# All v rows of gather passes 2, 4 and 6 to TensorE, in buffers of 4 picks of 32 tokens

## The chip, the cores and the metric

One core of one Trainium2 chip runs one program that is launched once. The time is device microseconds of that core, the median of the runs that were made; the trace is of one profiled execution of the same program. Engines are called PE (TensorE), PEld (its weight loads), DVE (VectorE), ACT (ScalarE), POOL (GpSimd) and SP (SyncE); the 16 DMA engines of the core are taken together.

## The reference, cut to what matters

A small model of 256 tokens, width 1024, all in float32: an mLSTM block, two PEER feed-forward layers, a latent attention block, gates, and a tail with a sparse attention, a convolution, a linear attention and a dense feed-forward. The change is in the PEER layers, which pick 128 single-neuron experts for each token (8 heads by 16 best) out of 16384:

```python
def peer_ffn(x, w_q, sub_keys, u, v):
    ...                     # scores of product keys, top 16 of each head: expert_idx, gates
    def expert_block(args):                       # a block of 128 tokens
        xb, eb, gb = args
        ub = jnp.take(u, eb, axis=0)              # 128 tokens x 128 picks x 1024
        act = jax.nn.gelu(jnp.einsum('thkd,td->thk', ub, xb), approximate=False)
        vb = jnp.take(v, eb, axis=0)              # the same number of rows of v
        return jnp.einsum('thk,thkd->td', gb * act, vb)
```

## The kernel before

The 256 tokens are two tiles of 128. With two layers, two tiles and the tables u and v there are eight **gather passes** of 128 gathers each, in the order (layer 0, tile 0, u), (0, 0, v), (0, 1, u), (0, 1, v), (1, 0, u), (1, 0, v), (1, 1, u), (1, 1, v). The code numbers them n = 0 to 7; the texts say pass 1 to pass 8, so that passes 2, 4, 6 are n = 1, 3, 5. One gather (`issue`, line 946) is one indirect DMA that POOL issues: partition p gets the row of 4 KB of the pick c of token p, so a buffer holds one pick of 128 tokens, 0.524 MB. There are `SLOTS` = 12 buffers, used in turn over all 1024 gathers; POOL waits, before gather i, until gather i - 12 has been used: on `row_used` if DVE used it, on `pe_used` if PE did. SP loads the dense weights in an order of their own into a ring of three buffers, beside the gathers.

A u row is one DVE instruction (`use_row`, line 991): the product with the token's x, which ACT has put into the PSUM tensor XP, summed to one number. A v row on DVE (lines 993 and 995) is XP = XP + row * gate. In passes 2, 4 and 6 (`SHARED`) half of the rows, four of every eight, are PE's: ACT writes a 128x128 diagonal matrix of the gates of this pick (`act_share`, line 1031, four of them in turn), and PE multiplies it with the row into two banks, accA and accB, by two matmuls of 512 columns (`pe_share`, line 1016 on; every float32 matmul is recorded as two MATMULs with a LDWEIGHTS each, so a buffer is four). Pass 8 is DVE's alone. `dve_sums` closes a pass: Y = ALPHA * X + XP, plus the two banks.

Around the passes the order is written out by hand in phases at whose ends PE, ACT and DVE meet. `weigh` lies in the last part of a u pass and turns the 128 sums of a token into gates in two halves of 64. `peer_route` projects the queries (four blocks of 32 matmul calls), scores them and picks the experts of the layer above (`picks`), with the v rows of passes 4 and 6 beside it: PE takes six rows, a block of queries, a block of scores, six rows, and so on. `peer_done` adds and normalises, and beside pass 2 it holds the scores and picks of the second tile. While DVE does its own steps, it takes a row now and then (`gather_some`), so that rows and steps alternate on it.

## Time and profile before

| | |
|---|---|
| median of 3 runs | 2252.76 us (2241.89 to 2260.28) |
| span of the profiled execution | 2259.6 us |
| instructions in it | 17114 |
| busy: PE, PEld, DVE, ACT, POOL | 1527.2, 879.4, 1450.5, 323.1, 985.0 us |
| DMA | 760.62 MB, of which gathers 536.94 MB |
| passes 1 to 8 begin at (first gather issued) | 208.45, 406.87, 595.72, 805.20, 1013.29, 1228.22, 1436.24, 1683.64 us |
| last gather issued | 1914.87 us |

The profiled execution has its span, 2259.6 us, as its time; it is 6.8 us (0.3%) above the median and 0.7 us below the longest of the three runs. Times inside the trace are counted from the start of the span.

### The profile page before, as it was taken

Reading aid. Unit: us, or ns where it says so; the run is one execution under the profiler, and the core shown is the slowest. Engines: PE = TensorE matmul, PEld = TensorE weight load, DVE = VectorE, ACT = ScalarE, POOL = GpSimd, SP = SyncE. Lnnn points to the kernel's source line nnn. Section 1 sums busy time; section 2 is a strip of 40 time slices with the busy share of each in tenths; the row PEclk is TensorE's granted clock in tenths of the full one; section 3 lists DMA queues with packets and bytes.
Section 4 is the critical chain, followed back from the end, with each engine's and each line's share of the span. In section 5 each row is a group of like instructions: output and inputs, shape, how many; then the busy total and the mean of one; then the engine's idle time right before and its main releaser. Section 6 shows DMA issues by size and latency. Waiting matters only on the chain. (4 is left out here: it accounts for less than half of the span.)

```text
span 2259.6 us, 17114 instructions
## 1 busy us (share of the span) xinstructions
PE 1527.2 (68%) x5282; PEld 879.4 (39%) x5282; DVE 1450.5 (64%) x3168; ACT 323.1 (14%) x778; POOL 985.0 (44%) x1058
## 2 busy tenths in 40 slices
PE   8987600467656539776573897666576656899998
PEld 7446600222225225422341552235252232376453
DVE  1236898779587875678688468786978676444101
ACT  1220100011112111111120111111321000123111
POOL 0102466667665555566455456653446444000000
PEclk9989855688867669987766899778767877899999
DMA  7436999999999999999999999999989999973672
GB/s 260 85 117 245 394 408 409 337 360 370 371 379 403 404 406 358 361 365 367 407 399 405 365 342 368 375 401 386 391 293 403 399 398 399 366 243 130 242 260 93
DMA packets 268005, 760.62 MB, mean 337 GB/s; under 512 B 21295, under 2 KB 46590, under 8 KB 267275
## 3 DMA queue, kind: packets, MB, share of 16 engines
q0 software_dynamic: 147456, 536.94, 61.8%
q1 hardware_dynamic: 120458, 222.60, 27.8%
q8 instruction: 43, 0.70, 0.1%
q14 instruction: 48, 0.39, 0.0%
HBM read 756.84 MB, written 2.62 MB: 336 GB/s over the span
## 5 line engine op out<-in xcount | busy, mean ns | idle before, releaser
L946 POOL DMA_INDIRECT ROWS<-in_peer_u,IDX x512 | 483.3, 944 | 455.5 <-DVE ROWS L991 266.9
L946 POOL DMA_INDIRECT ROWS<-in_peer_v,IDX x512 | 487.8, 953 | 357.2 <-PE bank L292 121.4
L991 DVE SCALAR_TENSOR_TENSOR ROWS<-ROWS,XP 128x1024 f32<-128x1024 f32 x512 | 602.3, 1215 | 23.7 <-issue 12.3
L995 DVE SCALAR_TENSOR_TENSOR XP<-ROWS,GATE,XP 128x1024 f32<-128x1024 f32 x316 | 405.8, 1284 | 155.9 <-DMA ROWS<-in_peer_v,IDX 133.7
L292 PE MATMUL bank<-ROWS,DG 128*128 128x512 f32 x774 | 380.0, 649 | 94.2 <-DMA ROWS<-in_peer_v,IDX 78.5
L292 PE MATMUL bank<-ring,XT 128*128 128x512 f32 (+6 forms) x912 | 392.7, 589 | 62.3 <-DMA ring<-in_ffn_w_up 32.0
L292 PEld LDWEIGHTS bank<-ring,XT 128*128 128x128 f32 x912 | 185.6, 214 | 249.9 <-issue 179.4
L292 PEld LDWEIGHTS bank<-ROWS,DG 128*128 128x128 f32 x774 | 157.5, 209 | 309.8 <-issue 201.8
L292 PE MATMUL bank<-XT,ring 128*128 128x128 f32 (+2 forms) x1504 | 209.4, 301 | 57.1 <-issue 27.4
L292 PEld LDWEIGHTS bank<-XT,ring 128*128 128x128 f32 (+1 forms) x1504 | 198.3, 204 | 71.8 <-issue 35.7
L307 PE MATMUL bank<-CN,X 128*128 128x128 f32 x128 | 27.1, 384 | 184.9 <-issue 90.7
L391 POOL TENSOR_TENSOR stat<-stat,CN 128x1 f32<-128x1 f32 x5 | 2.8, 552 | 304.6 <-DVE stat L1870 132.5
L292 PE MATMUL bank<-KEYT,QP 128*128 128x128 f32 x128 | 22.0, 333 | 162.9 <-DVEq L472 159.5
L1031 ACT ACTIVATE DG<-CN,GATE 128x128 f32<-128x128 f32 x192 | 71.0, 397 | 326.0 <-PE bank L292 198.6
L307 PEld LDWEIGHTS bank<-CN,X 128*128 128x128 f32 x128 | 22.5, 202 | 197.8 <-issue 197.8
L292 PE MATMUL bank<-ring,FT 128*128 128x512 f32 x132 | 67.2, 669 | 27.6 <-DMA ring<-in_ffn_w_down 19.9
L292 PEld LDWEIGHTS bank<-KEYT,QP 128*128 128x128 f32 x128 | 20.6, 246 | 164.9 <-issue 160.7
L1171 DVE MAX8 TV<-bank 128x8 f32<-128x128 f32 x64 | 14.3, 284 | 87.8 <-PE bank L292 86.7
L292 PE MATMUL bank<-VEC,CN 13*128 13x512 f32 x76 | 46.3, 756 | 30.6 <-DVEq L472 23.3
L292 PE MATMUL bank<-ROWS,XT 128*128 128x512 f32 (+3 forms) x176 | 65.3, 528 | 1.4 <-ACT XT L1847 1.4
L292 PEld LDWEIGHTS bank<-ring,FT 128*128 128x128 f32 x132 | 28.0, 217 | 65.6 <-issue 52.3
L886 POOL TENSOR_SCALAR_AFFINE_SELECT ROWS<-ROWS 128x128 f32<-128x128 f32 x16 | 4.3, 294 | 112.9 <-ACT ROWS L778 112.9
(408 smaller groups left out, 1461.6 us busy)
## 6 DMA issues: line engine op xcount, KB each, us to landing
ring<-in_peer_w_q SPq DMA_DIRECT2D x16, 2048.0 KB
ring<-in_ple_w_gate SPq DMA_DIRECT2D x9, 2048.0 KB
ring<-in_ffn_w_gate SPq DMA_DIRECT2D x8, 2048.0 KB
ring<-in_ffn_w_up SPq DMA_DIRECT2D x7, 2048.0 KB
ring<-in_a_w_in SPq DMA_DIRECT2D x6, 2048.0 KB
ring<-in_w_in SPq DMA_DIRECT2D x6, 2048.0 KB
ring<-in_ffn_w_down SPq DMA_DIRECT2D x6, 2048.0 KB
ROWS<-in_peer_u,IDX POOLq DMA_INDIRECT x512
```

The source lines that it names most:

```text
L292: return mm(out_, lhsT, rhs, start=start, stop=stop, skip_group_check=True)
L307: last = tr(b[:, j * P:(j + 1) * P], src[:, tt, (g + j) * P:(g + j + 1) * P], ident)
L391: G.tensor_tensor(cells, cells, CN[:, at:at + cells.shape[1]], ALU.pow).then_inc(*tick(name_out))
L886: ins = G.affine_select(block_, block_, [[1, P]], ALU.is_ge, zero, base=0, channel_multiplier=-1)
L946: G.indirect_dma_start(ROWBUF[slot(n, c)][:, :], None, tables[table], bass.IndirectOffsetOnAxis(IDX[:, tt, c:c + 1], axis=0)).then_inc(row ...
L991: V.scalar_tensor_tensor(row, row, 1.0, XP[:, :], ALU.mult, ALU.mult, accum_out=ACTV[:, tt, c:c + 1]).then_inc(row_used, 1)
L995: V.scalar_tensor_tensor(XP[:, :], row, gate, XP[:, :], ALU.mult, ALU.add).then_inc(row_used, 1)
L1031: A.activation(DG[tensor_used(n, x) % DIAGS][:, :], ident, ACT.Copy, scale=GATE[:, tt, c:c + 1]).then_inc(diag_ready, 1)
L1171: V.max(vals[:, k, at:at + 8], source(k)).then_inc(*tick("dve_step"))
```

## The change

Passes 2, 4 and 6 get another layout of a buffer and no longer use DVE or ACT for their rows.

- A gather of these passes takes, for partition 32k + t, the pick 4g + k of token 32q + t: four picks (k) of 32 tokens (q fixed), so that four buffers q = 0 to 3 hold four picks of all 128 tokens. The index table for it, `IDXV`, is made ahead of the pass: DVE writes the picks as floats once more (`IDXF`), PE moves them with 16 small matmul calls by 32 columns of the identity (`pe_to_quads`), and DVE copies them to integers. POOL waits for that (`picks_turned`) before the pass.
- The gates are moved in the same way in two halves, and DVE spreads them with four instructions of 128x1024 elements a pass (`dve_spread`): for each buffer a 128x32 matrix that has the gate of partition 32k + t in column t.
- PE multiplies such a 128x32 matrix with the buffer into the 32 partitions 32q to 32q + 31 of accA and accB. `pe_share` now goes by groups of four buffers: it waits until all four have landed, makes four calls into the four partition groups of accA, then four into those of accB, each of which raises `pe_used`.
- DVE takes no row of these passes, ACT makes no diagonals, and `dve_sums` adds ALPHA * X straight to the banks. ACT writes the x of the next u pass into XP as soon as the last u pass is used, and DVE takes two u rows before it adds.
- PE takes the first two groups in `weigh`, then four groups between two blocks of queries, and in `peer_done` of pass 2 it takes the rest after the scores.
- A part of the constants that only the first phase uses is loaded into the gather buffers instead of its own memory.

```diff
-        SHARED = (1, 3, 5)
+        BY_PE = (1, 3, 5)
         def by_pe(n, c):
-            return n in SHARED and c % (2 * RUN) >= RUN
+            return n in BY_PE
...
+                picks = IDXV if n in BY_PE else IDX
                 G.indirect_dma_start(ROWBUF[slot(n, c)][:, :], None, tables[table],
-                                     bass.IndirectOffsetOnAxis(IDX[:, tt, c:c + 1], axis=0)).then_inc(row_in[slot(n, c)], 16)
+                                     bass.IndirectOffsetOnAxis(picks[:, tt, c:c + 1], axis=0)).then_inc(row_in[slot(n, c)], 16)
...
+        def pe_to_quads(src, name):
+            m = src.shape[1] // GROUP
+            b = job(name)
...
+            for k in range(GROUP):
+                for q in range(GROUP):
+                    last = mul(b[QUAD * k:QUAD * k + QUAD, q:GROUP * m:GROUP], ident[:, QUAD * q:QUAD * q + QUAD],
+                               src[:, k:GROUP * m:GROUP], True, True)
...
+        def dve_spread(n, half):
...
+            for x in (2 * half, 2 * half + 1):
+                gates = result(name)[:, QUAD * (x % 2):QUAD * (x % 2) + QUAD]
+                V.tensor_tensor(spread(tt, x), con("spread").unsqueeze(1).broadcast_to([P, QUAD, QUAD]),
+                                gates.unsqueeze(2).broadcast_to([P, QUAD, QUAD]), ALU.mult).then_inc(spread_ready, 1)
...
+        def pe_share(n, g0=0, g1=PICKS // GROUP):
+            accs, tt = (result("accA"), result("accB")), passes[n][1]
+            for g in range(g0, g1):
...
+                PE.wait_ge(spread_ready, 4 * (n // 2) + x + 1)
+                weights = spread(tt, x)
+                for q in range(GROUP):
+                    PE.wait_ge(*arrived(n, GROUP * g + q))
+                for q in range(GROUP):
+                    to, row = slice(QUAD * q, QUAD * q + QUAD), ROWBUF[slot(n, GROUP * g + q)]
+                    last = mul(accs[0][to, :], weights[:, j + q, :], row[:, 0:512], first, end)
...
+                        mul(accs[1][to, :], weights[:, j + q, :], row[:, 512:1024], first, end).then_inc(pe_used, 1)
-                A.activation(DG[tensor_used(n, x) % DIAGS][:, :], ident, ACT.Copy, scale=GATE[:, tt, c:c + 1]).then_inc(diag_ready, 1)
...
         def dve_sums(n):
+            V.wait_ge(*nth("x_copied", 2))
+            gather_begin(n + 1)
+            gather_some(2)
             V.wait_ge(pe_used, tensor_used(n))
             for i, name in enumerate(("accA", "accB")):
                 V.wait_ge(bank_ready(name), turn(name))
-                y = Y[:, tt, i * 512:(i + 1) * 512]
-                V.tensor_tensor(y, y, result(name)[:, :], ALU.add).then_inc(bank_free(name), 1)
+                s = slice(i * 512, (i + 1) * 512)
+                V.scalar_tensor_tensor(Y[:, tt, s], X[:, tt, s], ALPHA, result(name)[:, :], ALU.mult, ALU.add).then_inc(bank_free(name), 1)
...
         def weigh(block, st, n):
+            if to_pe:
+                @block.tensor
+                def _(pe):
+                    for i, half in enumerate(halves):
+                        pe.wait_ge(*nth("gate_done", i + 1))
+                        pe_to_quads(GATE[:, tt, half], f"gv{i}")
+                    pe_share_begin(n + 1)
+                    pe_share(n + 1, 0, 2)
...
         def peer_route(block, st, l, tiles, tag, KEYT, KEYT1):
                 for e in range(5):
-                    if l == 1:
-                        pe_share(beside, 6 * e, 6 * e + 6)
+                    if l == 1 and e > 0:
+                        pe_share(beside, 4 * e - 2, 4 * e + 2)
...
                 if l == 1:
-                    pe_share(beside, 30)
+                    pe_share(beside, 18)
```

## Rows read from the trace of the kernel before

**Rows 1.** Page: busy engines; DMA share in tenths and GB/s, 40 slices
```profile
PE 1527.2 (68%) x5282; PEld 879.4 (39%) x5282; DVE 1450.5 (64%) x3168; ACT 323.1 (14%) x778; POOL 985.0 (44%) x1058
...
DMA  7436999999999999999999999999989999973672
GB/s 260 85 117 245 394 408 409 337 360 370 371 379 403 404 406 358 361 365 367 407 399 405 365 342 368 375 401 386 391 293 403 399 398 399 366 243 130 242 260 93
```

**Rows 2.** Windows, one for each pass 1, 2, 3, 4, 6, 8
```profile
core 0: us, PE busy (x) PEld busy (x) DVE busy (x) ACT busy (x) POOL busy (x), PEclk, DMA share, GB/s
208.45:406.87 198.42, 47.60 (x379) 45.60 (x378) 173.87 (x376) 9.98 (x17) 121.87 (x128) 0.63 1.03 400
406.87:595.72 188.85, 125.92 (x272) 54.40 (x272) 136.14 (x315) 24.63 (x65) 123.06 (x129) 0.85 0.95 356
595.72:805.20 209.48, 110.37 (x350) 65.63 (x350) 168.23 (x345) 30.74 (x66) 120.03 (x128) 0.69 1.02 395
805.20:1013.29 208.09, 154.03 (x536) 86.23 (x536) 134.54 (x316) 26.55 (x71) 122.11 (x129) 0.88 0.98 370
...
1228.22:1436.24 208.02, 157.38 (x536) 87.38 (x536) 135.29 (x317) 26.77 (x71) 122.65 (x129) 0.87 0.96 362
...
1683.64:1937.90 254.26, 156.45 (x322) 70.75 (x320) 182.43 (x168) 15.37 (x29) 119.95 (x128) 0.79 1.03 400
```

**Rows 3.** Windows: in pass 1, in pass 2, and the two parts of pass 4
```profile
320.00:360.00 40.00, 0.00 (x0) 0.00 (x0) 37.50 (x64) 0.26 (x1) 26.70 (x29) 0.50 1.03 409
...
430.00:440.00 10.00, 10.00 (x41) 5.93 (x40) 7.20 (x24) 1.55 (x4) 2.92 (x4) 0.98 0.64 220
...
805.00:945.00 140.00, 106.52 (x443) 67.46 (x444) 78.95 (x189) 16.87 (x45) 76.89 (x82) 0.86 0.98 376
945.00:1013.29 68.29, 47.52 (x95) 18.77 (x93) 55.79 (x127) 9.68 (x26) 45.22 (x47) 0.91 0.97 358
```

**Rows 4.** Page, costliest groups: busy us, mean ns of one, idle before
```profile
L946 POOL DMA_INDIRECT ROWS<-in_peer_v,IDX x512 | 487.8, 953 | 357.2 <-PE bank L292 121.4
L991 DVE SCALAR_TENSOR_TENSOR ROWS<-ROWS,XP 128x1024 f32<-128x1024 f32 x512 | 602.3, 1215 | 23.7 <-issue 12.3
L995 DVE SCALAR_TENSOR_TENSOR XP<-ROWS,GATE,XP 128x1024 f32<-128x1024 f32 x316 | 405.8, 1284 | 155.9 <-DMA ROWS<-in_peer_v,IDX 133.7
L292 PE MATMUL bank<-ROWS,DG 128*128 128x512 f32 x774 | 380.0, 649 | 94.2 <-DMA ROWS<-in_peer_v,IDX 78.5
```

**Rows 5.** Waits of POOL, pass 2, then pass 4: us, times, longest
```profile
POOL ROWS L946 <- PE bank L292: 21.3, 12, 5.3
...
POOL ROWS L946 <- PE bank L292: 48.7, 19, 8.9
```

**Rows 6.** Timeline of PE, then of POOL, in pass 2
```profile
485.44 4.88 PE L292 MATMUL bank<-ROWS,DG 128*128 128x512 f32 x11
492.53 7.13 PE L292 MATMUL bank<-ROWS,DG 128*128 128x512 f32 x16 [2.21 <-issue]
...
492.02 0.94 POOL L946 DMA_INDIRECT ROWS<-in_peer_v,IDX  x1 [0.30 <-issue]
497.06 0.94 POOL L946 DMA_INDIRECT ROWS<-in_peer_v,IDX  x1 [4.10 <-PE bank L292]
```

**Rows 7.** Timeline of PE and PEld, linear attention, first and second tile
```profile
1619.03 0.65 PE L292 MATMUL bank<-STB,QG 128*64 128x256 f32 x2
...
2041.77 0.65 PE L292 MATMUL bank<-STB,QG 128*64 128x256 f32 x4
...
2041.77 0.20 PEld L292 LDWEIGHTS bank<-STB,QG 128*64 128x64 f32 x4
```

**Rows 8.** Instructions nearest to the new ones: group by form, and timeline
```profile
L1224 DVE TENSOR_TENSOR QP<-HALFF,CN 128x1024 f32<-128x1024 f32 x16 | 19.5, 1218 | 0.8 <-remote 0.7
...
2040.74 1.10 PE L292 MATMUL bank<-GVS,AM 128*128 128x64 f32 x8
```

**Rows 9.** Timeline of PE in pass 4: a block of queries
```profile
838.19 6.53 PE L292 MATMUL bank<-XT,ring 128*128 128x128 f32 x57
```

More of the change, by code:

```diff
@@ L46 @@
 VECTORS = 13
-DIAGS = 4
+GROUP = 4
+QUAD = P // GROUP
 NH, NKV, HD = 8, 2, 64
@@ L122, in con @@
             at, n = cwhere[name]
+            if at >= early_at:
+                return CN_EARLY[0:rows_, at - early_at:at - early_at + n]
             return CN[0:rows_, at:at + n]
@@ L489, in end_phase @@
             base.update(count)
-            jobs.clear()
+            for name in [k for k in jobs if not (held and k in ("accA", "accB"))]:
+                del jobs[name]
         PE = nc.tensor
@@ L901, in build @@
         ACTV = sb("ACTV", [P, TT, PICKS], F32, peer_mem)
-        DG = [sb(f"DG{i}", [P, P], F32, peer_mem) for i in range(DIAGS)]
+        IDXF = sb("IDXF", [P, PICKS], F32, peer_mem)
+        IDXV = sb("IDXV", [P, TT, PICKS], I32, peer_mem)
         ROWBUF = [ROWS[:, s, :] for s in range(SLOTS)]
@@ new lines, in pe_turn_picks, with dve_turn_picks, spread @@
+        def pe_turn_picks(l, tt):
+            PE.wait_ge(S("pick_numbers"), 2 * (TT * l + tt) + 2)
+            pe_to_quads(IDXF[:, :], "turned")
+        def dve_turn_picks(l, tt):
+            V.wait_ge(bank_ready("turned"), turn("turned"))
+            V.tensor_copy(IDXV[:, tt, :], result("turned")[:, 0:PICKS]).then_inc(bank_free("turned"), 1)
+            V.wait_ge(bank_free("turned"), turn("turned"))
+            V.sem_inc(S("picks_turned"), 1)
+        def spread(tt, x):
+            part = Y[:, tt, :] if x == 2 else later["spread"][:, min(x, 2), :]
+            return part.rearrange("p (j t) -> p j t", t=QUAD)
@@ L1233, in best_pairs @@
                 step_done()
+                V.tensor_scalar(IDXF[:, ks], EX[:, 0, :], float(l * NEXP), None, ALU.add).then_inc(S("pick_numbers"), 1)
                 V.tensor_scalar(IDX[:, tt, ks], EX[:, 0, :], float(l * NEXP), None, ALU.add).then_inc(picks_ready, 1)
@@ L2813, in peers @@
                     phase(mla, tt, KNT, VM, KRT)
-                    phase(weigh, 2 + 2 * tt)
-                    phase(peer_route, 1, (tt,), f"1{tt}", KEYT1, None)
-                    phase(peer_done, 3 + 2 * tt)
+                    with ExitStack() as st:
+                        later["spread"] = sb("SPREAD", [P, 3, D], F32, st)
+                        phase(weigh, 2 + 2 * tt)
+                        phase(peer_route, 1, (tt,), f"1{tt}", KEYT1, None)
+                        phase(peer_done, 3 + 2 * tt)
             keys1_mem.close()
```

102 lines of the change are left out of this document (55 added, 47 removed).

## The prediction

> **What bounds the kernel now.** I read the page's slices first, then windows by pass, then who waits for whom. No engine is busy for more than 68% of the span, but the DMA line stands at 8 or 9 tenths in every slice from the fifth to the thirty-fourth [rows 1]: from the first gather at 208.45 us to the end of pass 8 the kernel is paced by transfers. The windows tell how well. Passes 1, 3 and 8, whose rows are DVE's alone, move 395 to 400 GB/s at a share of 1.02 or 1.03; passes 2, 4 and 6, which share their rows between DVE and PE, move 356, 370 and 362 GB/s at 0.95 to 0.98 [rows 2]. The best stretch moves 409 [rows 3], which is 0.524 / 409 = 1.28 us a gather. So the time that this change can win is the difference of these rates in three passes, and the work that it takes off DVE is not itself on the path.
>
> The ceiling of it: a pass's bytes are its window by its rate, 67.2, 77.0 and 75.3 MB. At 403 GB/s (between 400 and 409) they take 167, 191 and 187 us, where they take 188.9, 208.1 and 208.0 now [rows 2]. That is 22 + 17 + 21 = **60 us**, and no version with the same bytes wins more in these passes.
>
> Why the transfers fall short: POOL waits for PE to give back buffers, 21 us in pass 2 and 49 us in pass 4 [rows 5]. PE takes 380.0 / 192 = 1.98 us for a buffer [rows 4], 7.13 us for a run of four at the full clock [rows 6], and between runs it has a block of queries, 6.5 us for the bulk of one [rows 9]; at the start of pass 2 such a wait leaves the DMA engines at 0.64 and 220 GB/s for 10 us [rows 3]. A second cause is POOL itself. An issue takes 0.94 us and 0.30 us lie before the next [rows 6], so POOL gives at most one gather in 1.24 us, against 1.28 us of transfer: once the queue has run low it hardly fills again. And some of its pauses are not about buffers. The one before 497.06 us is put down to PE, but counting issues against uses, the buffer needed is that of gather 47, a PE row, and PE was through with it at 485.44 + 4.88 = 490.3 us, 6.7 us earlier [rows 6]. By the same count over the whole trace, pauses without a missing buffer cost 21 us in pass 2, 10 in pass 4 and 17 in pass 6; buffers cost 9, 39 and 33. I don't know what makes the former.
>
> **The change, part by part.**
>
> DVE loses 3 x 64 = 192 rows of 1.284 us [rows 4], 247 us. In passes 2, 4, 6 DVE is busy for 135 of 189 to 208 us [rows 2] and falls to some 55 plus the new steps. This is no gain by itself: what was late there was the buffer.
>
> PE had 64 buffers a pass, about 127 us at 1.98. It now has 128 buffers in 32 groups of 16 MATMULs of the same 512 columns. If the four partition groups ran one after the other, a group would cost the 7.13 us of [rows 6]. The trace has one place where matmuls write two partition groups of a bank side by side: the linear attention makes one call of 64 output rows for the first tile, and for the second tile two calls into partitions 0 to 63 and 64 to 127. The first takes 0.65 us for 2 MATMULs, the second 0.65 us for 4 [rows 7]. Two groups cost what one costs, in float32, in one bank. For four groups there is no row; the bounds are 7.13 / 4 = 1.8 us if all overlap and 7.13 / 2 = 3.6 us if only two do. I take 1.8 to 2.4, near full overlap; what matters is that both ends are below the 4 x 1.28 = 5.1 us in which four buffers land. So PE needs 58 to 115 us a pass for rows, less than now, and stops being late. At a granted clock of 0.50 (1.2 GHz) the ends double to 3.6 and 7.1 us; the latter alone would be too slow, but PE without pauses has clocks of 0.86 to 0.98 here [rows 3].
>
> A rule of the Trainium skill speaks against it. TensorE: Matmul & The Clock Gate, Part 3, says that weight loads overlap matmuls in flight only when the row group differs, and here all four groups use all rows. The loads of the two-group case run under its matmuls, 0.20 us of loads inside 0.65 us [rows 7], so this trace does not agree. By the rule sixteen loads at 0.20 / 4 = 0.05 to 0.1 us would add 0.8 to 1.6 us to a group, as an estimate, and the sum would stay, since 4 us is still below 5.1. The same part gives 2.38 times the throughput for three column groups; that would be about 3 us for a group, again with the sum unchanged.
>
> Between two blocks of queries PE now has 16 buffers, 7 to 10 us, and queries and scores of about 9, so 16 to 19 us, while 16 buffers and 2 MB of weights take 16 x 1.28 + 5 = 25.5 us to land. The longest absence of PE, some 10 us, is covered by the eight buffers that are then under way or to be filled (8 x 1.28 = 10.2 us, plus the weights). So the 39 and 33 us of buffer waits go, in as far as the DMA engines can use it.
>
> New on DVE: four spreads a pass, 12 x 1.22 us by the nearest row, the one-hot products of the picks [rows 8], 15 us in all. Two of them lie before the last 60 u rows of passes 1, 3, 5, with a wait for PE's 32 small matmuls of at most 0.14 us [rows 8], up to 4.4 us less the two rows taken meanwhile. DVE gets some 4 us late and wins 0.14 us a row back (a u row recurs after 1.14 us when nothing is missing); 12 buffers cover what is left. Bounds: 0 and 3 x 4 = 12 us. I take 2. Were DVE as late as in the middle of pass 7, all 12 would count.
>
> At the turn from u to v, PE starts only after the second half of the gates, and only when four rows have landed. The last u row of pass 1 is used at about 423 us, gate and move take about 4 us, the first group about 3.6 at the low clock: buffers come back at about 431 us, four at once, while the transfers under way last until about 437. Bounds 0 and 5 us a pass, I take 1. In return the 5 us wait near 430 us of pass 2 falls away [rows 3].
>
> ACT loses 192 diagonals, which nobody misses. The second write of the picks, the float copy and the turned indices lie on DVE and PE ahead of passes that start 100 us later or more; in front of pass 1 they add 0.3 us. POOL waits for `picks_turned`, with everything behind it on its queue, but by then this is long raised. POOL issues the same 1024 gathers of the same bytes, and SP one more transfer of the constants, under the first phase.
>
> **The sum.** What decides is how much of the 60 us POOL lets through. Where weights share the engines (until about 945 us in pass 4, 140 us at 376 GB/s [rows 3]) few gathers are needed and the DMA bound is reached: 140 x (1 - 376/403) = 9 us, and in pass 6, at 362 over the whole pass [rows 2], 14. In the stretches of gathers alone, all of pass 2 and the last 68 us of passes 4 and 6, POOL's own pauses stay: pass 2 becomes 128 x 1.24 + 21 = 180 us and wins 9; the two ends run at 358 now, and take 0 to 8 us less each, I take 4. That is 9 + 9 + 14 + 8 = 40. The earlier start of u rows at the end of passes 2, 4, 6 (DVE takes two before it waits for PE) gives perhaps 1 each, and the spreads and the turns cost 2 + 3: **38 us**. The profiled span of 2259.6 becomes 2221.6; against the median of 2252.8 it is **2215 us**.
>
> **The rivals.**
>
> *The full ceiling.* The pauses that have no missing buffer may come from the alternation with PE: pass 3 has few of them. Then 60 less 5 gives 2198 us. For it: pass 1 runs at 409 for 40 us with POOL undisturbed. Against: pass 1 has such pauses too, and its rate sinks towards its end.
>
> *POOL is the bound anyway.* If POOL's pauses grow where it no longer waits for buffers, to what pass 2 shows today (356 GB/s), passes 4 and 6 hardly move, and the spreads and turns cost their 12 and 15 us bounds in part: 10 us less, 2243 us, within 1%.
>
> *The partition groups don't overlap.* Two groups of 64 do; four of 32 might not. Then a group costs 7.13 us and a pass 32 x 7.13 = 228 us, plus 5 in pass 2, and plus PE's other 27 us and the drains, 32, in passes 4 and 6: 233 + 260 + 260 = 753 against 605 us now, 148 us more, **2401 us**. It decides as soon as a group with its share of queries takes over 6.4 us, which is 5.1 us and a quarter of the weights. This is also the case in which the change does not do what it says.
>
> **How the numbers follow.** The middle case 0.57 (2200 to 2228), the full ceiling 0.11, POOL bound 0.21 (2231 to 2262), no overlap 0.08 (2330 to 2420), and 0.03 for something slower by 20 to 60 us at the turns. A measurement here can tell 1%, 22 us, from nothing. Below 2230: 0.70. Within 1%: 0.19. Above 2275: 0.11. The range leaves out no overlap and a little on either side: 2190 to 2258.
>
> **What would show it.** In the profile after: L995 with 128 rows instead of 320; MATMULs of 128*32 with four starting nearly together and a group in about 2 us; POOL's waits for PE in pass 4 falling from 49 us to under 10; windows of passes 2, 4, 6 of about 180, 195 and 190 us at 375 to 400 GB/s; passes 1, 3, 5, 7, 8 as long as before. The prediction is wrong if a group takes over 5 us, if POOL's issues come more than 1.45 us apart without waits, or if the last u rows of passes 3 and 5 are used so late that the DMA share falls at the turn.

## The result, and the profile after

The changed kernel takes 2269.12 us (median of 7 runs, 2261.97 to 2278.42), the kernel before 2259.91 us in 7 runs beside it. The ratio is 1.007, with an interval of 1.0049 to 1.0091: slower by 0.7%. 2215 us was forecast, 54 us less than measured, and 2269 lies above the range. The profiled execution took 2261.97 us (span 2260.2), the shortest of the seven.

The page after, busy engines and GB/s in 40 slices, against [rows 1]:

```profile
PE 1431.8 (63%) x6338; PEld 796.0 (35%) x6338; DVE 1233.9 (55%) x2996; ACT 253.1 (11%) x586; POOL 983.4 (44%) x1058
...
GB/s 259 83 131 240 395 408 390 341 363 372 376 376 404 405 370 376 353 365 349 405 403 397 371 329 372 367 399 399 391 307 403 401 398 401 382 252 120 245 257 105
```

DVE lost 217 us of work and PE 95, and the rates (GB/s) are those of before. The windows of passes 1 to 8, in the columns of [rows 2]:

```profile
207.19:409.86 202.67, 51.92 (x443) 49.38 (x442) 173.11 (x380) 10.06 (x17) 122.23 (x129) 0.64 1.02 392
409.86:596.47 186.61, 94.78 (x556) 24.57 (x560) 64.58 (x255) 1.38 (x3) 121.42 (x128) 0.73 0.97 361
596.47:812.56 216.09, 116.24 (x426) 69.60 (x416) 168.41 (x346) 29.62 (x64) 120.29 (x129) 0.66 1.02 395
812.56:1019.07 206.51, 118.95 (x824) 58.17 (x824) 66.95 (x261) 4.85 (x9) 121.44 (x128) 0.78 0.96 363
1019.07:1236.27 217.20, 125.35 (x446) 73.82 (x438) 169.57 (x346) 31.32 (x64) 120.27 (x129) 0.67 1.00 390
1236.27:1442.45 206.18, 123.07 (x808) 58.88 (x808) 66.67 (x261) 4.85 (x9) 122.07 (x128) 0.75 0.95 359
1442.45:1681.49 239.04, 144.80 (x652) 99.81 (x652) 192.51 (x472) 48.99 (x143) 121.60 (x129) 0.69 1.01 380
1681.49:1917.40 235.91, 151.14 (x305) 69.11 (x306) 168.89 (x158) 15.37 (x29) 119.20 (x127) 0.78 1.02 393
```

Passes 2, 4 and 6 were to fall to 180, 195 and 190 us at 375 to 400 GB/s. They take 186.6, 206.5 and 206.2 us at 361, 363 and 359, some 2 us less each than [rows 2]. Passes 1, 3 and 5 are 4.3, 6.6 and 2.3 us longer, pass 7 8.4 us shorter, and the last gather is issued at 1917.40 us instead of 1914.87.

The work itself is as the change says. Costliest groups of the page, against [rows 4]:

```profile
L955 POOL DMA_INDIRECT ROWS<-in_peer_v,IDXV x384 | 364.9, 950 | 240.2 <-issue 97.0
...
L298 PE MATMUL bank<-ROWS,SPREAD 128*32 128x512 f32 (+1 forms) x1158 | 192.0, 784 | 151.0 <-DMA ROWS<-in_peer_v,IDXV 131.7
...
L1006 DVE SCALAR_TENSOR_TENSOR XP<-ROWS,GATE,XP 128x1024 f32<-128x1024 f32 x127 | 163.7, 1289 | 65.8 <-DMA ROWS<-in_peer_v,IDX 63.8
...
L298 PE MATMUL bank<-ROWS,Y 128*32 128x512 f32 x384 | 70.5, 856 | 64.6 <-DMA ROWS<-in_peer_v,IDXV 57.6
```

The two PE lines are one kind of work: a quarter of the weights lies in the memory of Y. Together they are PE's 96 groups of 16 MATMULs.

Waits of POOL in pass 2, then pass 4, against [rows 5]:

```profile
POOL ROWS L955 <- remote: 19.4, 11, 3.2
POOL ROWS L955 <- PE bank L298: 11.8, 10, 4.2
...
POOL ROWS L955 <- PE bank L298: 43.8, 13, 10.7
```

The 48.7 us of waits in pass 4 were to fall under 10 and are 43.8, in fewer and longer pieces (13 up to 10.7 us, where there were 19 up to 8.9). POOL's pauses are of two kinds, and two stretches show them. First PE, in pass 4, timeline:

```profile
843.01 5.36 PE L298 MATMUL bank<-ROWS,SPREAD 128*32 128x512 f32 x48
858.28 3.64 PE L298 MATMUL bank<-ROWS,SPREAD 128*32 128x512 f32 x16 [9.91 <-DMA ROWS<-in_peer_v,IDXV]
861.85 7.82 PE L298 MATMUL bank<-XT,ring 128*128 128x128 f32 x64
869.51 1.06 PE L298 MATMUL bank<-KEYT,QP 128*128 128x128 f32 x8
870.50 5.36 PE L298 MATMUL bank<-ROWS,SPREAD 128*32 128x512 f32 x48
```

PE does three groups in 5.36 us, since they have long landed, and then waits 9.91 us for the fourth, whose gathers POOL could issue only from 845.19 us on, with buffers of the first of the three. With the fourth done at 861.9 PE goes away for queries and scores until 870.5, and gives nothing back before 872.4. POOL fills the four buffers of that fourth group (862.15 to 865.88) and stands still until 872.67. So such a block finds four free buffers, not eight. POOL's gaps at these places, from issue to issue, are 6.6, 6.8, 9.9 and 11.7 us in pass 4 and 6.6, 8.2, 11.2 and 11.8 us in pass 6, against 1.245 us without a wait.

Second, POOL, DVE and PE in pass 2, where no queries are:

```profile
496.14 0.94 POOL L955 DMA_INDIRECT ROWS<-in_peer_v,IDXV  x1 [0.30 <-issue]
499.94 0.94 POOL L955 DMA_INDIRECT ROWS<-in_peer_v,IDXV  x1 [2.85 <-remote]
...
494.04 0.27 DVE L1241 FIND_INDEX8 BI<-BV,SC 128x8 uint32<-128x112 f32 x1
499.57 0.23 DVE L1266 TENSOR_TENSOR GATE<-BV 128x64 f32<-128x64 f32 x1 [5.26 <-remote]
...
492.56 1.92 PE L298 MATMUL bank<-ROWS,SPREAD 128*32 128x512 f32 x16 [1.97 <-DMA ROWS<-in_peer_v,IDXV]
497.67 3.52 PE L298 MATMUL bank<-ROWS,SPREAD 128*32 128x512 f32 x16 [3.18 <-DMA ROWS<-in_peer_v,IDXV]
```

The gather at 499.94 needs the first buffer of the group that starts at 492.56 and by its MATMUL records ends at 494.48. This is a pause "without a missing buffer", as the prediction has them. The trace also records when semaphore updates arrived, and there the four updates of this group stand at 499.68 to 499.80 us, 5.2 us after the records' end. POOL goes on 0.26 us later. DVE, which waits only for its own FIND_INDEX8, goes on at 499.57, when that one's update stands at 499.55. So no sign is left of POOL pausing by itself: of its 105 pauses over 0.45 us in passes 2, 4 and 6 of both kernels, 100 end within 0.35 us of an update of a semaphore that it waits for. The end of a MATMUL in the trace is modelled; the update is what a waiting engine sees.

### The profile page after: what moved, and what is told of

It is laid out like the page before. It is cut to its first block and busy times, and to the rows that moved or that the text cites. A ratio compares the mean times of both kernels' runs of the same rounds, so it can differ in the third digit from the quotient of the medians.

```text
span 2260.2 us, 18704 instructions
## 1 busy us (share of the span) xinstructions
PE 1431.8 (63%) x6338; PEld 796.0 (35%) x6338; DVE 1233.9 (55%) x2996; ACT 253.1 (11%) x586; POOL 983.4 (44%) x1058
## 5 line engine op out<-in xcount | busy, mean ns | idle before, releaser
L955 POOL DMA_INDIRECT ROWS<-in_peer_v,IDXV x384 | 364.9, 950 | 240.2 <-issue 97.0
L298 PE MATMUL bank<-ROWS,SPREAD 128*32 128x512 f32 (+1 forms) x1158 | 192.0, 784 | 151.0 <-DMA ROWS<-in_peer_v,IDXV 131.7
L298 PE MATMUL bank<-XT,ring 128*128 128x128 f32 (+2 forms) x1504 | 216.1, 307 | 44.7 <-issue 19.6
L298 PEld LDWEIGHTS bank<-XT,ring 128*128 128x128 f32 (+1 forms) x1504 | 203.8, 211 | 66.1 <-issue 35.2
L1006 DVE SCALAR_TENSOR_TENSOR XP<-ROWS,GATE,XP 128x1024 f32<-128x1024 f32 x127 | 163.7, 1289 | 65.8 <-DMA ROWS<-in_peer_v,IDX 63.8
L955 POOL DMA_INDIRECT ROWS<-in_peer_v,IDX x128 | 120.1, 939 | 117.0 <-DVE XP L1006 96.9
L298 PE MATMUL bank<-GATE,CN 128*32 128x16 f32 x192 | 8.0, 217 | 224.0 <-issue 191.8
L298 PEld LDWEIGHTS bank<-ROWS,SPREAD 128*32 128x32 f32 x1158 | 45.1, 129 | 285.1 <-issue 282.0
L298 PE MATMUL bank<-ROWS,Y 128*32 128x512 f32 x384 | 70.5, 856 | 64.6 <-DMA ROWS<-in_peer_v,IDXV 57.6
L298 PEld LDWEIGHTS bank<-GATE,CN 128*32 128x32 f32 x192 | 7.3, 153 | 227.0 <-issue 192.4
```

What stands on the lines that cost most here:

```text
L298: return mm(out_, lhsT, rhs, start=start, stop=stop, skip_group_check=True)
L955: G.indirect_dma_start(ROWBUF[slot(n, c)][:, :], None, tables[table], bass.IndirectOffsetOnAxis(picks[:, tt, c:c + 1], axis=0)).then_inc(r ...
L1006: V.scalar_tensor_tensor(XP[:, :], row, gate, XP[:, :], ALU.mult, ALU.add).then_inc(row_used, 1)
```

## The experiments

Eighteen kernels were run in five batches; in each batch the kernel before ran beside them on the same chip. It takes 2253 to 2260 us in two batches (and in the measurement above), and 2192 to 2194 in the other three. That is a condition of the batch and not of a kernel; some expectations put it down to the chip, but one chip showed both. I call the two **2260 batches** and **2194 batches** (the expectations say "call"). In all ten profiles of the first kind (the two given ones too) DVE stands idle over 1 us for its own last update, 6 to 17 times, as before 499.57 above; in all ten of the second kind it never does. Kernels are compared within a batch, by the ratio to the kernel before.

The two kinds of profile also differ in how complete they are. In the ten of 2194 batches all updates of PE and DVE but 3 at most are recorded, and 18679 to 18711 updates by landing DMAs; in the ten of 2260 batches 76 to 87% of those of DVE and only 10008 to 11050 of the latter. Where an engine goes on right behind a recorded update, as above, the lateness is real. But counts of late updates in 2260 profiles are rough, and whether the slower condition has its cause in the recording of the profile itself is a rival that no run here tests.

| kernel | ratio, interval | passes 2, 4, 6, us | 1 + 3 + 5 | 7 + 8 |
|---|---|---|---|---|
| **2260 batches:** before | 1 | 188.8, 208.1, 208.0 | 622.8 | 478.6 |
| after | 1.0070, 1.0049 to 1.0091 | 186.6, 206.5, 206.2 | 636.0 | 474.9 |
| e1_fine | 0.9949, 0.9929 to 0.9968 | 187.0, 191.5, 192.2 | 640.3 | 475.8 |
| e2_late_spread | 1.0069, 1.0043 to 1.0096 | 187.5, 213.6, 213.6 | 631.9 | 474.2 |
| e4_half_rows | 0.9972, 0.9947 to 0.9996 | 185.0, 199.6, 200.8 | 635.1 | 480.7 |
| e5_fine_late | 0.9938, 0.9914 to 0.9962 | 193.1, 194.0, 192.7 | 632.2 | 477.1 |
| s4_after | 1.0067, 1.0040 to 1.0094 | 186.7, 209.4, 207.5 | 637.3 | 474.5 |
| s3_warm | 1.0077, 1.0050 to 1.0103 | 190.2, 205.7, 204.3 | 636.6 | 477.5 |
| s2_no_use | 1.0161, 1.0119 to 1.0203 | 207.1, 210.8, 210.1 | 645.5 | 475.7 |
| s1_no_use_all | 1.0429, 1.0387 to 1.0471 | 207.1, 233.2, 232.7 | 643.0 | 483.2 |
| **2194 batches:** r1_before | 1.0002, 0.9986 to 1.0019 | 169.6, 189.4, 190.0 | 612.6 | 482.4 |
| r2_after | 0.9994, 0.9980 to 1.0007 | 171.1, 186.4, 189.4 | 613.6 | 477.3 |
| r3_fine | 0.9978, 0.9962 to 0.9994 | 171.2, 185.1, 184.5 | 614.4 | 480.8 |
| e3_row_by_row | 1.0015, 0.9999 to 1.0031 | 171.5, 187.4, 187.2 | 614.2 | 478.7 |
| e6_weights_by_act | 0.9979, 0.9963 to 0.9995 | 171.0, 187.6, 187.6 | 609.6 | 479.5 |
| e8_warm | 1.0009, 0.9997 to 1.0021 | 171.5, 188.9, 186.8 | 616.0 | 478.5 |
| r4_no_use | 1.0000, 0.9986 to 1.0014 | 164.1, 186.2, 188.3 | 621.2 | 478.8 |
| e9_no_use | 1.0006, 0.9994 to 1.0018 | 163.2, 189.3, 189.5 | 619.3 | 477.9 |
| t1_one_signal | 0.9977, 0.9962 to 0.9992 | 171.8, 186.7, 185.4 | 612.1 | 476.3 |
| t2_few_signals | 0.9989, 0.9973 to 1.0004 | 170.9, 185.2, 185.2 | 614.4 | 479.6 |

Lengths of passes run from first gather to first gather, in each one's profiled execution; pass 8 to the last gather. They scatter from one profile to the next: s4_after is the changed kernel once more, and its passes 2, 4 and 6 differ by 0.1, 2.9 and 1.3 us from the row "after". The kernels with no_use in their names leave out nearly all of the v sums of pass 2 (s1_no_use_all of passes 2, 4 and 6). r3_fine is e1_fine again, and e5, e6, s1, t1 and t2 contain its edit, e4 the like.

**First batch (a 2260 batch).** The theory was that PE's absence during whole query blocks holds buffers back; the rival, that POOL's issue and the transfers set the pace anyway.

```diff
# e1_fine
-                        pe_share(beside, 4 * e - 2, 4 * e + 2)    # four groups, then a block of queries
...
+                            queries_between(w, tiles[0], e, lambda s: pe_share(beside, 4 * e + s + 2, 4 * e + s + 3))
```

> One group of four buffers after every column of a query block (a quarter of a block) in passes 4 and 6, instead of four groups between whole blocks; nothing else changed. Theory A (PE's absence during a whole block holds the buffers back: the four long pauses of POOL in each of these passes, 6.6 to 11.8 us, are waits for PE): these pauses fall below 4 us, passes 4 and 6 go from 206 us to about 190 us each, the kernel to about 34 us less than the changed kernel, 2235 us where that has 2269. Rival B (POOL's issue of 1.24 us and the transfers pace these passes anyway, the pauses only move): passes 4 and 6 stay within 5 us of 206, the kernel within 10 us of the changed kernel.

```diff
# e2_late_spread; e5_fine_late is this and e1_fine together
                 if to_pe:
-                    gather_some(2)
+                    gather_some(8)
                     dve_spread(n + 1, 0)
```

> Eight u rows instead of two between the product of the first half of the gates and the first two spreads on DVE; nothing else changed. Theory A (DVE waits for PE's 32 small matmuls, 7.4 us in pass 1 and 2.7 us in pass 3, and this lengthens passes 1, 3 and 5): the waits before the spreads go, passes 1, 3 and 5 are shorter by 4, 3 and 1 us, the kernel by 5 to 12 us. Rival B (twelve buffers hide the wait): no pass changes by over 2 us and the kernel by under 4 us.

> The edits of the finer interleaving and of the later first spreads together, all rows of passes 2, 4 and 6 on PE. Theory A: the sum of the two, about 40 us less than the changed kernel. Rival B: within 10 us of the changed kernel. If one of them only moves time to the other, the sum is smaller than the two apart by over 5 us.

```diff
# e4_half_rows, with DVE's rows added in dve_sums as before,
# the groups between columns as in e1_fine, and the late first spreads
-            return n in BY_PE
+            return n in BY_PE and c % 8 >= 4
```

> Half of the rows only: of each eight picks of passes 2, 4 and 6 DVE takes the first four one by one, as in the kernel before, and PE the second four as one group with four partition groups of 32; groups lie between the columns of the queries, and the first spreads wait eight rows. Theory A (buffers that come back only four at once and only from PE are the loss): POOL's pauses for PE in pass 2 fall from 24.6 us to under 12 and in passes 4 and 6 from 42 to 48 us to under 25; passes 2, 4 and 6 are shorter than in the kernel before by 8, 15 and 15 us, the kernel by 25 to 40 us than the one before. Rival B (transfers and POOL's issue pace it anyway): within 10 us of the kernel before.

e1_fine is 23 us below the changed kernel by the medians (2245.67 against 2269.12 of the measurement above; the ratios give 27). Windows of its passes 4 and 6:

```profile
817.43:1008.93 191.50, 118.94 (x808) 56.23 (x808) 66.51 (x261) 4.85 (x9) 120.37 (x128) 0.82 1.00 385
...
1227.89:1420.09 192.20, 120.09 (x812) 56.15 (x816) 66.95 (x261) 4.85 (x9) 122.08 (x129) 0.80 1.00 386
```

Timeline of PE in its pass 4:

```profile
841.88 1.92 PE L298 MATMUL bank<-ROWS,SPREAD 128*32 128x512 f32 x16
843.74 2.43 PE L298 MATMUL bank<-XT,ring 128*128 128x128 f32 x16
846.41 1.97 PE L298 MATMUL bank<-ROWS,SPREAD 128*32 128x512 f32 x16 [0.24 <-issue]
```

The same work, interleaved by the column, gives 363 and 359 GB/s back to 385 and 386, and each pass is 14 to 15 us shorter, as theory A had it (190 us); from issue to issue the gaps behind query blocks are 4.7 us at most instead of 11.8. The kernel gains 23 to 27 us of the 34 expected. e2_late_spread gains nothing, as rival B had it for the kernel: the waits before the first spreads go in passes 3 and 5 but stay in pass 1 (8.3 us), passes 1, 3 and 5 fall by 4 us in all, and passes 4 and 6 grow by 7 each. Part of that is only moved: the gap of 6.7 us before the first gather of pass 4 in the profile after (4.8 in pass 6) comes a few gathers later, inside the pass. e5_fine_late is within 5 us of e1_fine, not 40 us below the changed kernel but 30. e4_half_rows wins 7 to 9 us in each of passes 4 and 6 against the kernel before, half of what e1_fine wins there, and 0.3% as a kernel (rival B): giving DVE half of the rows back is no better than spacing PE's groups well. In pass 2 all six kernels have 25 to 29 us of pauses, whoever uses the rows (before 28.8, after 25.6, e1_fine 26.7, e2_late_spread 27.3, e4_half_rows 25.5, e5_fine_late 28.6): the cause there is in none of their differences.

**Second batch (a 2194 batch).**

```diff
# e3_row_by_row
                     last = mul(accs[0][to, :], weights[:, j + q, :], row[:, 0:512], first, end)
-                for q in range(GROUP):
-                    to, row = slice(QUAD * q, QUAD * q + QUAD), ROWBUF[slot(n, GROUP * g + q)]
                     ...      # accs[1], in the same turn of q
```

> The same matmuls of a group in another order: both halves of a buffer's columns behind each other, then the next buffer (partition group 0, 0, 1, 1, 2, 2, 3, 3 instead of 0, 1, 2, 3, 0, 1, 2, 3). Theory A (partition groups overlap only where matmuls that follow each other in the queue write different groups): a group takes 4.8 to 5.6 us at the full clock instead of 1.9, twice that at the lower one; that is over the 5.1 us in which four buffers land, PE becomes the bound of passes 2, 4 and 6, and the kernel is 50 to 250 us slower. Rival B (the order doesn't matter): 1.9 us a group, the kernel within 8 us of the changed one.

```diff
# e6_weights_by_act, on e1_fine; DVE's dve_spread is gone
+            for c in range(c0, c1):
+                x, j = divmod(c, QUAD)
+                A.activation(spread(tt, x)[:, j, :], con("spread"), ACT.Copy, scale=ACTV[:, tt, c:c + 1]).then_inc(spread_ready, 1)
```

> The finer interleaving, and the weights no longer made by DVE in twelve products of 1.22 us but by ACT, a column at a time (128 operations of 128x32 a pass); PE's turns of the gates stay. Theory A (the two or four spreads and the waits for PE's 32 small matmuls on DVE lengthen passes 1, 3 and 5 by 4 to 8 us each against the kernel before): passes 1, 3 and 5 come back to within 3 us of 198, 210 and 215 us, and the kernel takes 8 to 16 us less than with the finer interleaving alone. Rival B (other parts of the change, or the fuller queue itself, lengthen them): within 4 us of the finer interleaving alone.

```diff
# e8_warm (and s3_warm), on the changed kernel
+                if not end and (n == 1 or g >= 18):
+                    for _ in range(3):
+                        mul(accs[0][0:14, :], con("pad"), CN[:, 0:512], False, False)
```

> The changed kernel with three matmuls that add zeros behind every group in pass 2 and behind groups 18 to 30 of passes 4 and 6, so that PE has no long pauses there. Theory A (the lower clock, 3.6 us a group for 1.9, is what gives buffers back late in the stretches of gathers alone): the granted clock rises above 0.9, POOL's pauses in pass 2 fall from 25 us to under 12, the pass is 10 us shorter. Rival B (the late returns have another cause): the pass stays within 4 us of 187 us, or gets longer by the work added.

```diff
# e9_no_use (and r4_no_use, s2_no_use), on the changed kernel
-                if m >= 0 and by_pe(m, h):
+                if m == 1 and h < PICKS - GROUP:
+                    G.wait_ge(*arrived(m, h))
+                elif m >= 0 and by_pe(m, h):
...                  # and in pe_share, once the group has landed
+                if n == 1 and not end:
+                    PE.sem_inc(pe_used, GROUP)
+                    continue
```

> The changed kernel, but of pass 2 only the last group of four rows is multiplied (the v sum of the first token tile in the first layer is left out except for four of its 128 picks), and POOL waits in this pass only until the gather of twelve rows earlier has landed. Theory A (consumers give buffers back late; without them POOL never pauses): POOL issues every 1.24 us, pass 2 takes 128 x 1.28 = 164 us at most, 20 us less than now, at 400 GB/s or more. Rival B (the transfers themselves or POOL have hiccups that would come anyway): pauses of 3 to 4 us every 12 to 16 gathers stay and the pass keeps 180 to 187 us.

Two theories fell, those of e3_row_by_row and e6_weights_by_act. In e3_row_by_row a group takes 1.95 us at the full clock (PE timeline, pass 2):

```profile
457.38 1.95 PE L298 MATMUL bank<-ROWS,SPREAD 128*32 128x512 f32 x16 [1.70 <-DMA ROWS<-in_peer_v,IDXV]
462.41 3.46 PE L298 MATMUL bank<-ROWS,SPREAD 128*32 128x512 f32 x16 [3.08 <-DMA ROWS<-in_peer_v,IDXV]
```

The order of the eight matmuls of a group doesn't matter; rival B holds. And pass 2 takes 171 to 172 us in e3_row_by_row, e6_weights_by_act and e8_warm alike, which is no merit of theirs; that could only be read with the kernel before on the same footing. So e8_warm decides nothing about the clock here. e6_weights_by_act shortens passes 3 and 5 by 2.5 us each against r3_fine (208.5 and 209.1 against 211.2 and 211.6), but the ratio is that of r3_fine: rival B. In e9_no_use hardly a wait of POOL is left in pass 2 (2 us in all), the pass takes 163 us, as theory A had it, and the kernel is not faster.

**Third batch (a 2194 batch)**, on one footing: both kernels, e1_fine and e9_no_use again.

> The kernel before once more, for its profile on the chip of this call. The four runs before this call came from a chip on which the kernel before takes 2194 us instead of 2260, and on which a changed kernel issues the gathers of pass 2 with 10 us of pauses instead of 25. If theory A holds (the 3 to 4 us pauses in stretches of gathers alone belong to one chip, whatever kernel runs), the kernel before shows the same difference: on a chip of 2194 us its pass 2 takes 170 to 176 us instead of 189, on one of 2260 us again 187 to 190. Rival B (they belong to the changed kernel's way of using rows): pass 2 of the kernel before keeps 186 to 190 us on either.

> The changed kernel once more on the chip of this call. Theory A: on a chip of 2194 us pass 2 takes 171 us and passes 4 and 6 some 188 us; against the kernel before on the same chip the sum of passes 2, 4 and 6 is within 10 us, and the ratio is 1.000 to 1.004; on a chip of 2260 us the ratio is 1.004 to 1.009. Rival B (without the hiccups of the other chip the change brings what was forecast): ratio below 0.990.

> The finer interleaving of queries and groups once more. On a chip of 2260 us: 0.995 of the kernel before, as measured. On a chip of 2194 us: theory A (PE's absence in the query blocks is a loss on any chip): passes 4 and 6 fall from 188 us to under 180 each, ratio 0.991 to 0.995. Rival B (there the transfers already fill these passes, 400 GB/s): ratio 0.998 to 1.002.

> The kernel in which only the last four rows of pass 2 are multiplied (the v sum of the first token tile in the first layer is left out except for four picks) once more. On a chip of 2194 us pass 2 takes 163 us again. On one of 2260 us: theory A (the pauses are late returns of buffers, even where the chip itself makes them late): pass 2 takes 163 to 168 us and has no pauses above 3 us. Rival B (that chip's transfers or POOL have hiccups of their own): 178 us or more, with pauses.

Windows of passes 2, 4 and 6 of r1_before:

```profile
399.19:568.82 169.63, 117.27 (x269) 52.42 (x270) 134.66 (x318) 24.82 (x63) 122.87 (x129) 0.89 1.02 404
...
779.42:968.80 189.38, 148.55 (x533) 81.54 (x534) 133.84 (x316) 26.57 (x70) 123.07 (x129) 0.89 1.02 403
...
1178.38:1368.42 190.04, 149.47 (x536) 81.91 (x536) 134.70 (x317) 27.31 (x71) 124.20 (x128) 0.90 1.02 401
```

The same of r2_after:

```profile
399.73:570.82 171.09, 85.91 (x544) 22.65 (x544) 67.36 (x261) 1.37 (x3) 120.72 (x129) 0.80 1.02 406
...
781.90:968.29 186.39, 110.02 (x808) 52.58 (x808) 66.74 (x261) 4.74 (x9) 120.87 (x129) 0.79 1.01 396
...
1179.24:1368.68 189.44, 113.35 (x808) 53.23 (x808) 66.77 (x261) 4.74 (x9) 122.09 (x129) 0.76 1.01 393
```

Theory A of r1_before holds: here the kernel before moves 401 to 404 GB/s in the three passes. The 60 us between it and the ceiling are not there to be won, because the same program already has them. The changed kernel has 0.9994 of its time (r2_after, theory A again within 0.001), and r3_fine 0.9978, which is rival B: PE's absence in the query blocks costs some 3.5 us here, where it cost 23 to 27. The order of PE's work is the same as in the profile after, but POOL's pauses in passes 4 and 6 are 30 and 33 us, none over 7.3, where they are 49 and 50 there, up to 11.8; in the kernel before (r1_before) they are 30 and 31. So in neither condition did the change take pauses away. Windows of passes 2 and 3 of r4_no_use:

```profile
398.02:562.14 164.12, 7.42 (x64) 7.13 (x64) 67.47 (x261) 1.37 (x3) 121.02 (x128) 0.51 1.03 409
562.14:780.65 218.51, 112.51 (x414) 67.31 (x414) 171.18 (x346) 29.72 (x64) 119.83 (x128) 0.65 1.03 402
```

What pass 2 wins, pass 3 gives back: 164.1 + 218.5 = 382.6 us, against 171.1 + 211.1 = 382.2 in r2_after, both at 405 GB/s over the two. In this condition no consumer of pass 2 costs the kernel anything. Of 96 groups in r2_after, none has its first update over 1 us behind the end of its MATMUL records; in the profile after it is some 28 of 96, some 75 us in sum, and in s4_after some 24 of 96, 53 us, by the updates that are recorded.

**Fourth batch (a 2260 batch).**

```diff
# s1_no_use_all, on e1_fine: as e9_no_use, in passes 2, 4 and 6, for PE too
-                if m >= 0 and by_pe(m, h):
+                if m in BY_PE and h < PICKS - GROUP:
+                    G.wait_ge(*arrived(m, h))
+                elif m >= 0 and by_pe(m, h):
```

> The finer interleaving, and of passes 2, 4 and 6 only the last group of four rows is multiplied (the v sums of three of the four tiles are left out except for four of 128 picks); POOL waits in these passes only until the gather of twelve rows earlier has landed, so no consumer can hold it. Theory A (on a chip where the kernel before takes 2194 us the transfers are at their ceiling already, over 400 GB/s, and what a pass wins the next one gives back): passes 2, 4 and 6 fall to 164, 180 and 180 us, passes 3, 5 and 7 grow by about as much, and the kernel stays within 12 us of the finer interleaving. On a chip of 2260 us the late returns cost real time: there the kernel falls by 30 to 60 us. Rival B (buffers held by PE still cost on any chip): 20 us or more less than the finer interleaving on either.

> Only the last four rows of pass 2 are multiplied, as in the earlier run, for a profile on the chip of this call. On a chip of 2260 us: theory A (late returns of buffers) 163 to 168 us for pass 2, no pauses; rival B (hiccups of the transfers or of POOL) 178 us or more with pauses of 3 to 4 us. On a chip of 2194 us: 164 us again.

> Three matmuls that add zeros behind each group in the stretches of gathers alone, as in the earlier run. On a chip of 2260 us: theory A (a lower clock of PE makes the returns late) pass 2 under 177 us; rival B (another cause) 183 to 192 us. On a chip of 2194 us: 171 us again.

> The changed kernel once more, the measure for the other three on this chip. On a chip of 2260 us: pass 2 187 us with seven or more pauses above 3 us, ratio 1.004 to 1.009; on one of 2194 us: 171 us, ratio 0.998 to 1.001.

Here both theories on the late returns missed. Without any wait for a consumer, and without most of PE's matmuls, the kernel gets **slower**: with pass 2 alone by 25 us (2294.59 us against 2269.79 of s4_after), with all three passes by some 108 us against e1_fine, on which it is built (2352.71 us; the ratios are 1.0429 and 0.9949). The windows of passes 2 and 3 of s2_no_use:

```profile
415.40:622.45 207.05, 11.40 (x82) 8.51 (x82) 48.36 (x202) 1.38 (x3) 119.87 (x128) 0.51 0.83 331
622.45:842.41 219.96, 111.37 (x396) 67.68 (x396) 183.80 (x399) 29.47 (x64) 120.18 (x129) 0.65 1.00 383
```

POOL issues its 128 gathers at 1.24 us each, the last at 574.84 us, (159 us for the 128 instead of 187), and then waits 46.7 us for the picks of the second tile. Those are late on DVE. Its longest waits in 420 to 620 us of s2_no_use:

```profile
DVE Y L1056 <- remote: 63.2, 1, 63.2
DVE TV L1244 <- remote: 43.5, 4, 20.7
```

The first of these is for PE's 32 small matmuls of the gates. Their records end at 432.08 us, and DVE goes on at 493.10, 61 us later.

Two windows there:

```profile
470.00:520.00 50.00, 6.43 (x32) 6.24 (x32) 5.56 (x22) 1.12 (x2) 37.69 (x41) 0.53 1.03 409
...
597.00:622.00 25.00, 1.90 (x14) 0.52 (x6) 23.67 (x106) 0.00 (x0) 0.00 (x0) 0.50 0.00 0
```

For 50 us DVE is busy 5.6 us, from 597 us on 23.7 of 25. In r4_no_use, the same program in a 2194 batch, DVE writes the first half of these picks, for which POOL waits, at 460 us instead of 622, and its longest wait before they are all made is 7.3 us. The recorded updates of DVE's own step semaphore in s2_no_use, in us:

```
... 526.61 528.01 529.41 | 535.01 537.81 542.70 543.41 544.81 554.61 560.21 565.81 571.41 572.81 ...
... 585.40 586.80 588.20 589.60 591.01 593.80 595.91 597.31 597.34 597.73 598.00 598.27 598.86 ...
```

But for 542.70 and 595.91 they come 1.40 us apart or a multiple of it, also after the last gather of the pass has landed at 586.43 us, until 597.31; from then on they come as fast as DVE works. This is a guess from incomplete records (1612 of DVE's 1950 updates are in this profile): it looks as if the updates of DVE, and those of PE beside them, stood in a queue that lets one through each 1.40 us while gathers run without a gap, and for 11 us after. s3_warm lifts the mean clock (0.806 against 0.774 of s4_after, over the kernel) and leaves the pauses of pass 2 at 28 us: the pass takes 190.2 us, rival B. The late returns are not a matter of PE's clock.

**Fifth batch (a 2194 batch).** If the updates stand in a queue, fewer of them should be late less.

```diff
# t1_one_signal, on e1_fine; tensor_used counts groups
-                        mul(accs[1][to, :], weights[:, j + q, :], row[:, 512:1024], first, end).then_inc(pe_used, 1)
+                        last = mul(accs[1][to, :], weights[:, j + q, :], row[:, 512:1024], first, end)
+                        if q == GROUP - 1:
+                            last.then_inc(pe_used, 1)
```

> The finer interleaving, and PE signals each group of four buffers once, on its last matmul, instead of once for each buffer (96 semaphore updates instead of 384); POOL could use them only together anyway, they came 43 ns apart. Theory A (in calls where the kernel before takes 2250 to 2260 us, updates from PE and DVE pass only every 1.40 us while gathers are issued back to back, and queue up): with three of four updates of PE gone the pauses of POOL in pass 2 fall from 26 us to 10 to 18 us, and the kernel is 10 to 25 us faster than with the finer interleaving alone (0.984 to 0.990 of before); in a call where the kernel before takes 2194 us, where updates pass at once, nothing changes (0.997 to 1.000). Rival B (the pauses have nothing to do with the number of updates): ratio as for the finer interleaving alone, 0.993 to 0.997 in the one kind of call.

```diff
# t2_few_signals, on t1_one_signal
                 for k in ks:
-                    V.max(vals[:, k, at:at + 8], source(k)).then_inc(*tick("dve_step"))
+                    last = V.max(vals[:, k, at:at + 8], source(k))
+                last.then_inc(*tick("dve_step"))
```

> The same, and DVE's pick steps (the four or eight MAX8, MATCH_REPLACE8 and FIND_INDEX8 of a batch) signal once for each batch instead of once for each operation. Theory A: DVE's updates stand in the same queue, so the pauses beside the picks in passes 2, 4 and 6 shrink further and the pick steps themselves wait less; 5 to 15 us less than with PE's signals reduced alone in a call of 2250 to 2260 us, within 3 us of it in one of 2194 us. Rival B: no difference between the two in either.

Nothing changes against r3_fine, as both theories say for a 2194 batch, so this pair decides nothing. Whether fewer updates help in a 2260 batch stays open.

## Why the prediction was wrong

**What bounds the kernel now:** right in outline, transfers pace it, and wrong in the ceiling. "The time that this change can win is the difference of these rates" took 356 to 370 GB/s for a property of the kernel before. In r1_before it moves 404, 403 and 401. In the profiled condition the difference is real, but the same kernel takes 56 us less for these passes in a 2194 batch: most of the difference has its cause in the condition and not in who uses the rows.

**"A second cause is POOL itself":** right in the 1.24 us that an issue takes, wrong in the pauses. Those "without a missing buffer" (21, 10 and 17 us) were counted against the modelled ends of MATMULs. Against the recorded updates nearly all are waits for PE and DVE like the others. With every issue that comes over 1.45 us after the one before counted, POOL's pauses in passes 2, 4 and 6 are 29, 49 and 49 us before and 26, 49 and 50 after.

**PE's cost of a group:** right. 1.92 us at the full clock and 3.5 to 3.6 us at the lower, against 1.8 to 2.4 taken and 3.6 to 7.1 as ends; 7.13 us was the row before [rows 6]. The rival without overlap is out. On the rule of the Trainium skill weighed there (TensorE: Matmul & The Clock Gate, Part 3), that loads overlap only where the row group differs: the trace after does not agree. These loads use all rows, and 16 MATMULs with their 16 loads take 1.92 us (492.56 above).

**The step that failed: "So the 39 and 33 us of buffer waits go".** By the count of the prediction itself they are 32 and 35 us after. It rested on "The longest absence of PE, some 10 us, is covered by the eight buffers that are then under way or to be filled". That would hold if PE came back with buffers landing all along. In the written order it takes three landed groups at once, waits for the fourth while POOL stands dry, and leaves right after it (843.01 to 870.50 above); only four buffers carry the block. e1_fine, with the same work and another order, shows it: 15 and 14 us less in these passes, 23 to 27 us in all. So the coarse order is about half of the 54 us between 2215 and 2269. In the profiled executions 39 us are missing (2260.2 against 2221.6), and they add up: passes 4 and 6 take 12 and 16 us more than forecast, pass 2 7, passes 1, 3 and 5 11, and passes 7 and 8 and what lies around the gathers 7 less. The other 15 us are mostly the luck of the profiles: the one after is the shortest of its seven, the one before lay above the median of its three. Even with the order mended the kernel wins 0.5% in this condition, not 1.7. And the order is a loss of this size only in a 2260 batch: in a 2194 batch it is 0.0016 of the time, 3.5 us.

**The stretches of gathers alone:** "pass 2 becomes 128 x 1.24 + 21 = 180 us". It takes 186.6. The pauses cost 26 us where 21 were taken: nearly all of the 29 us of before were waits for late updates, the part put down to buffers too, and a faster PE does not shorten those. PE's group at 492.56 was worth 1.92 us and returned its buffers after 7.1.

**Spreads:** taken as 2 us with bounds 0 and 12. Passes 1, 3 and 5 grew by 4.3 + 6.6 + 2.3 = 13 us in the profiled execution, and by 1.0 us in r2_after against r1_before. The first spread waits 7.40 us for PE's 32 small matmuls in pass 1, whose records end 8.4 us before it starts; in r2_after all waits before the 12 spreads are 4.5 us together, against 25.4. So the spreads cost little, and with the late updates before them they cost the upper bound. e2_late_spread shows that moving the first two later does not help the kernel.

**Ends of passes:** "1 each" for the earlier u rows. Pass 7 is 8.4 us shorter and pass 8 is 4.7 longer, in 2194 batches 10.3 and 5.2. e4_half_rows, which closes a pass as the kernel before does, has 251 and 230 us, which points to the new closing. Why pass 8 gives half of it back was not tested.

**The rivals:** "POOL is the bound anyway" came nearest, "passes 4 and 6 hardly move, and the spreads and turns cost", at 2243 us. Its number missed by 26 us, and its reason is not what was found: POOL waits, it does not bound. The chances do not quite follow from the cases either: the cases give 0.68 below 2230 and 0.21 within 1%, where 0.70 and 0.19 are stated.

**Still open:** what sets the condition of a batch and whether the recording has a part in it, whether there is a place that passes an update each 1.40 us, and whether t1_one_signal or t2_few_signals help there. The best kernel seen is e1_fine, or e5_fine_late within its error: 0.994 to 0.995 of before in 2260 batches; e1_fine has 0.998 in 2194 batches.

## What to carry to other kernels

Count waits against what the waiting engine sees, the semaphore updates, and not against modelled ends of matmuls; a pause "without a reason" is then a late signal with a place. Look first whether the updates are all recorded. When an engine serves a ring of buffers beside other work, its speed matters less than its longest stretch away and what has landed when it leaves: here one group after each quarter of the other work was better than four groups and then all of it, by 23 to 27 us in one condition and 3.5 in the other. And take a second profile of the kernel before beside the first experiments: a shortfall that the same program doesn't show on another day is no gain to plan with.

## What was not expected of the hardware

- Four matmuls of 128x32 weights into four partition groups of a bank run fully together in float32, whether they alternate between the groups (1.92 us for 16 MATMULs) or stay in one for two matmuls (1.95 us).
- By the times of their packets, an indirect gather lands 5.2 us after its issue in the mean of pass 2 after, where mostly three or four others are under way, and 10.8 us in that of r4_no_use, where mostly eight are. POOL issues one each 1.243 us at best.
- One program on one core takes 2194 or 2260 us by the batch. The slower condition shows as late updates of PE and DVE in the semaphore records, 61 us late at worst, and most where POOL never pauses, and as records that are missing. There, freeing POOL of its waits for consumers cost 25 us in one pass and some 108 in three. That POOL's pauses are what lets the other engines' updates through fits this, but no run tried it by itself: these kernels also leave out PE's matmuls.
